# Scores of the first two groups moved into the input products of three attentions, and the conv taps cut in four

## The chip, the cores and the metric

The kernel runs on one core of a Trainium2 chip. The metric is the device time of one execution in microseconds; lower is better. Each number of the trace comes from one profiled execution.

## The reference, cut to what matters

Two transformer blocks run one after the other on 256 rows of width 1024, all in float32. The first has a sliding-window attention beside a differential one, a cross attention over a memory of 256 rows, and a feed-forward net. The second has two layers with modulation from a condition vector; layer 0 mixes a short convolution with a latent attention (MLA), layer 1 is a sparse attention with three branches (NSA). The three attentions that the change touches:

```python
def cross_attention(h, m, w_q, w_kv, w_o):
    q = (h @ w_q).reshape(Bn, S, CROSS_HEADS, CROSS_HEAD_DIM)        # 4 heads of 256
    ...
    s = jnp.einsum('bshd,bmhd->bhsm', q, k) * CROSS_HEAD_DIM ** -0.5
    p = jax.nn.softmax(s, axis=-1)

# MLA: 8 heads, 64 + 32 columns, causal; beside it the short convolution
u, gate_c, gate_b, cq, ckv, kr = jnp.split(h @ w_in, ...)
y_conv = gate_b * short_conv(gate_c * u, conv_w)                      # 3 taps, 512 channels

# NSA: 16 heads of 64, three branches
return gb[..., 0:1] * o_c + gb[..., 1:2] * o_s + gb[..., 2:3] * o_w   # compressed, selected, window
```

## The kernel before, in words

Everything of size runs on TensorE as a product of split numbers: each weight unit (128 x 2048, 1 MB) is loaded by DMA into `raw`, ScalarE copies it into a rounded high part `whi` (`split_hi`, L1101), VectorE subtracts it to get the low part `wlo` (`split_lo`, L1118), and `three` (L1162 to L1164) does three matmuls for each product. There are three such buffers (four in some stages), and a unit is split two or three units ahead of its use. While the products run, VectorE also forms the modulation vectors (`ada_terms`, L2175 and L2181): eight partial sums per part of `ada_w`, held in the buffers of `qT` and `pT`, and TensorE adds them over the partitions (`ada_out`, L1309).

The order of work on each engine is fixed by a list of stages that `make_plan` writes. Every engine walks the same list and issues its own part of each stage; engines wait for each other through semaphores only, so whatever stands behind a waiting instruction waits too. `linear` writes a product x @ w unit by unit; its argument `inner` hangs stages behind a unit. `T` counts the rounds of a pair of PSUM banks in which TensorE transposes (`turn`, L1166 to L1171, four transposes of 128 x 128 a round); a round needs the bank of the round before last emptied, by ScalarE ("A", L1806) or VectorE ("D", L2257).

An attention works in groups of heads and query rows. For each group TensorE computes scores (L1422 cross, L1426 MLA, L1437 NSA, L1414 compressed) into one of two pairs of banks, VectorE takes the row maxima (`smax`, L2292 to L2301; for NSA it adds the mask first and copies the scores to SBUF), ScalarE the exponentials with their sums (`exps`, L1832), TensorE transposes the result (`turn_probs`), ScalarE copies it to `pT` (L1840), and TensorE multiplies with the values (L1491). The loop of `attend` (L1474) does in step i: scores of group i + 1, values of group i - 2, transposes of group i - 1, and then the stages that are nested at i. Groups use three buffers for their exponentials in turn (`probs`). Before the first scores TensorE waits until every round in the stage's list `turned` has been emptied.

Before the change the three attentions open like this. Cross: the query product `w_cq` runs (four units), the partial sums of the modulation end behind it, then all eight rounds of query and key transposes, then the loop. MLA: the input product has eight units, the last six for the convolution; query transposes stand behind unit 5, key transposes and the whole of `conv_taps` (L2417 to L2420: sixteen VectorE operations) behind unit 6, then unit 7 and the loop. NSA: behind unit 5 the hidden layer of the compressed keys and values (`cmp_hid`), behind unit 6 their transposes and half of the query rounds, behind unit 7 `cmp_out` (its two rounds are emptied by VectorE: `kcz` L2486, `kz` L2492) and the other half, then the loop.

## Time and profile before

| | us |
|---|---|
| three timed runs, median (lowest, highest) | 1523.01 (1517.4, 1527.09) |
| the profiled execution's own time | 1518.52 |
| its span, first to last instruction | 1516.7 |
| TensorE busy | 1456.2 (96%) |
| VectorE busy | 1053.7 (69%) |
| ScalarE busy | 729.2 (48%) |
| mean granted clock of TensorE | 0.990 |

Cross opens at some 207 us of the span, MLA at 712, NSA at 1216. In the rows below PE is TensorE, DVE is VectorE, ACT is ScalarE. A timeline row gives the start, the time taken, the engine and line, the operation, output<-input, and how many instructions are merged in it; in square brackets stands how long the engine was idle before it and what it waited for. An fp32 matmul of scores or values shows as two records.

### The profile page before, as it was taken

To read this page: it belongs to the slowest core of one execution; us is meant where nothing else is said; L and a number is where in the kernel's file an instruction comes from. 1 tells how busy PE (TensorE), PEld (TensorE's weight loads), DVE (VectorE), ACT (ScalarE), POOL (GpSimd) and SP (SyncE) were. 2 spreads that over 40 slices of the span, in tenths; PEclk is the share of its full clock that TensorE was granted. 3 is DMA by queue.
4 is the path that set the end of the run, shared out by engine and by line. 5 is a ranking of instruction groups with operands and counts; after the bars stand their busy time and mean duration, and the time that the engine had idled before them with its cause. 6 is when DMAs were issued, how large, how long until landed. Compare 5 with 4: busy or idle time off the path is not lost.

```text
span 1516.7 us, 18742 instructions
## 1 busy us (share of the span) xinstructions
PE 1456.2 (96%) x7206; PEld 1197.3 (79%) x7206; DVE 1053.7 (69%) x1432; ACT 729.2 (48%) x1101; POOL 75.9 (5%) x133
## 2 busy tenths in 40 slices
PE   8997999999999999998999999899999989999998
PEld 7885777888877888887778888688887867788886
DVE  4897565877777777666477767777777678775544
ACT  6545545444454434364464333544435765554342
POOL 7200000000000000010000000000000000000000
PEclk9999999999999999999999999999999999999999
DMA  8870434687856888634368888588883710566560
GB/s 299 281 249 29 167 111 167 232 302 270 272 189 220 302 271 273 225 123 161 105 234 290 280 264 274 171 281 270 284 280 121 243 46 1 180 193 202 188 208 28
DMA packets 189087, 314.21 MB, mean 207 GB/s; under 512 B 6896, under 2 KB 100440, under 8 KB 189000
## 3 DMA queue, kind: packets, MB, share of 16 engines
q1 hardware_dynamic: 148800, 232.87, 46.9%
q10 hardware_dynamic: 38408, 75.65, 13.7%
q0 software_dynamic: 1792, 4.51, 1.0%
q8 instruction: 58, 0.95, 0.3%
q14 instruction: 29, 0.24, 0.0%
HBM read 311.92 MB, written 1.07 MB: 206 GB/s over the span
## 4 chain that ended last, share of the span: by engine, by line
PE 82%; DVE 9%; ACT 5%; issue 3%; DMA 1%; POOL 1%; ACTq 0%; POOLq 0%; DVEq 0%
PE ps L1162 24%; PE ps L1164 24%; PE ps L1163 23%; PE ps L1171 5%; PE ps L1491 2%; PE ps L1309 2%; DVE wlo L1118 1%; PE ps L1437 1%; DVE rmax L2295 1%; ACT sp L1832 1%; DVE tmp L1986 1%; ACT whi L1101 1%; DVE xn L1933 1%; DVE x L1941 0%; DVE wide L1118 0%
## 5 line engine op out<-in xcount | busy, mean ns | idle before, releaser
L1118 DVE TENSOR_TENSOR wlo<-raw,whi 128x2048 fp32r<-128x2048 f32 (+2 forms) x168 | 381.4, 2273 | 153.1 <-ACT whi L1101 153.0
L1162 PE MATMUL ps<-whi,aT 128*128 128x512 f32 (+3 forms) x1000 | 400.5, 401 | 10.6 <-DVE aTl L1974 6.1
L1164 PE MATMUL ps<-wlo,aT 128*128 128x512 f32 (+3 forms) x1000 | 388.9, 389 | 0.0
L1163 PE MATMUL ps<-whi,aTl 128*128 128x512 f32 (+3 forms) x1000 | 387.7, 388 | 0.0
L1101 ACT ACTIVATE whi<-raw 128x2048 fp32r<-128x2048 f32 (+2 forms) x169 | 319.5, 1895 | 82.7 <-DVE prow L2181 35.9
L1162 PEld LDWEIGHTS ps<-whi,aT 128*128 128x128 f32 x1000 | 188.6, 189 | 54.1 <-issue 11.3
L1164 PEld LDWEIGHTS ps<-wlo,aT 128*128 128x128 f32 x1000 | 188.5, 188 | 39.8
L1163 PEld LDWEIGHTS ps<-whi,aTl 128*128 128x128 f32 x1000 | 189.2, 189 | 34.3
L1778 ACT ACTIVATE hT<-ps 128x256 fp32r<-128x256 f32 (+1 forms) x102 | 42.2, 414 | 340.6 <-PE ps L1171 172.4
L1162 PE MATMUL ps<-whi,hT 128*128 128x512 f32 (+1 forms) x364 | 141.1, 390 | 1.4 <-ACT z L1756 1.4
L1164 PE MATMUL ps<-wlo,hT 128*128 128x512 f32 (+1 forms) x364 | 138.4, 382 | 0.0
L1163 PE MATMUL ps<-whi,hTl 128*128 128x512 f32 (+1 forms) x364 | 138.1, 381 | 0.0
L1118 DVE TENSOR_TENSOR wide<-raw,wide 128x2048 fp32r<-128x2048 f32 (+1 forms) x46 | 104.4, 2269 | 31.6 <-ACT wide L1101 31.6
L1101 ACT ACTIVATE wide<-raw 128x2048 fp32r<-128x2048 f32 x45 | 86.2, 1916 | 13.3 <-DVE prow L2181 5.0
L2181 DVE SCALAR_TENSOR_TENSOR qT<-qT,cact 128x512 f32<-128x512 f32 x108 | 80.9, 749 | 2.6
L2228 DVE TENSOR_TENSOR hTl<-ps,hT 128x256 fp32r<-128x256 f32 (+1 forms) x102 | 46.7, 458 | 50.8 <-ACT hT L1778 50.8
L1794 ACT ACTIVATE sp<-ps 128x256 f32<-128x256 f32 x88 | 33.5, 382 | 96.9 <-PE ps L1164 96.9
L1162 PEld LDWEIGHTS ps<-whi,hT 128*128 128x128 f32 (+1 forms) x364 | 67.1, 184 | 15.5 <-issue 2.1
L1164 PEld LDWEIGHTS ps<-wlo,hT 128*128 128x128 f32 (+1 forms) x364 | 67.0, 184 | 14.2
L1162 PE MATMUL ps<-wide,aT 128*128 128x512 f32 (+1 forms) x184 | 74.2, 403 | 3.4 <-DVE aTl L1974 2.1
L1163 PEld LDWEIGHTS ps<-whi,hTl 128*128 128x128 f32 (+1 forms) x364 | 67.2, 185 | 12.7
L1162 PE MATMUL ps<-wide,hT 128*128 128x512 f32 (+1 forms) x192 | 73.3, 385 | 0.0
(271 smaller groups left out, 2030.3 us busy)
## 6 DMA issues: line engine op xcount, KB each, us to landing
raw<-in_ff_w SPq DMA_DIRECT2D x176, 512.0 KB, 4.8
raw<-in_ff_w SPq DMA_DIRECT2D x44, 1024.0 KB, 5.1
qT<-in_ada_w ACTq DMA_DIRECT2D x36, 1024.0 KB, 6.7
pT<-in_ada_w ACTq DMA_DIRECT2D x36, 1024.0 KB, 7.2
raw<-in_w_up SPq DMA_DIRECT2D x16, 1024.0 KB, 5.8
raw<-in_w_down SPq DMA_DIRECT2D x16, 1024.0 KB, 5.1
raw<-in_w_in SPq DMA_DIRECT2D x9, 1024.0 KB, 9.8
raw<-in_w_ckv SPq DMA_DIRECT2D x8, 1024.0 KB, 5.5
```

What stands on the lines that cost most here:

```text
L1101: act.activation(hi_of(u), raw_of(u), ACT.Copy).then_inc(w_hi, 1)
L1118: dve.tensor_tensor(lo_of(u), raw_of(u), hi_of(u).bitcast(F32), ALU.subtract).then_inc(w_lo, 1)
L1162: pe.matmul(out_ap, hi, w, start=start, stop=False)
L1163: pe.matmul(out_ap, lo, w, start=False, stop=False)
L1164: return pe.matmul(out_ap, hi, wl, start=False, stop=stop)
L1171: last = pe.transpose(tbank(t)[0:m, col:col + kp], src, ident[0:kp, 0:kp])
L1309: last = pe.matmul(tbank(t)[:, c:c + 1], asum[:, k * P:(k + 1) * P], ones[:, 0:1], start=True, stop=True)
L1491: last = pe.matmul(o[:, i * dv:(i + 1) * dv], pT[:, n % 2, i * g["nkc"] + kc, :], zt[:, kc, v0:v0 + dv], start=kc == 0, stop=kc == g["nkc" ...
L1778: act.activation(hT[:, e["base"]:e["base"] + nk, e["tt"] * P:(e["tt"] + 1) * P], tbank(e["t"])[:, 0:nk * P].rearrange("p (a b) -> p a b", ...
L1794: act.activation(part(tt)[:, 0:HB2], bank[:, 0:HB2], ACT.Silu).then_inc(r_ready, 1)
L2181: ins = dve.scalar_tensor_tensor(asum if q == KC - 1 else w, w, c, before, ALU.mult, ALU.add)
L2228: dve.tensor_tensor(hTl[:, k0:k0 + nk, to], tbank(e["t"])[:, 0:nk * P].rearrange("p (a b) -> p a b", b=P), hT[:, k0:k0 + nk, to].bitcast(F ...
```

## The change

It takes the scores, maxima and exponentials of the first groups out of the loop and hangs them into the input product as a stage of their own, `attend_head`. TensorE does the scores of groups 0 and 1 there, VectorE and ScalarE the maxima and exponentials of the first `ahead` groups: two in cross and MLA, one in NSA.

- Cross: two rounds of keys are turned behind unit 1 of `w_cq`; a round of keys, two of queries and the head behind unit 2; a round of keys and two of queries remain behind unit 3. The third buffer for exponentials moves to another part of `z`.
- MLA: queries and keys are turned together behind unit 5, the head stands behind unit 6. `conv_taps` is cut in four portions (product, first tap, second tap, third tap) nested at steps 0 to 3 of the loop; the gate moves from step 1 to step 3.
- NSA: groups alternate, two of the first 128 query rows and two of the last (heads 0 to 7, then 8 to 15). The first half of the queries is turned ahead of the hidden columns behind unit 6, with the head behind it; the second half moves into step 1 of the loop, and group 4 waits for it. Group 1 holds its exponentials in `gbc`.

```diff
-        self.keys_turned = r[-2:]
+        self.keys_turned = r
...
-    p.linear(A["w_cq"][0], D, D, "z", "w_cq", flush=3)
-    p.turned("qk_cross", 8, ["A", "D"] * 4)
-    attend("cross", list(p.keys_turned), A["w_co"][0], None, {4: first_half(), 5: early(0), 6: rest_then_early})
+    def cross_head():
+        cross_turn((0, 1), (2,))
+        attend_head("cross", cross, 2)
+
+    p.linear(A["w_cq"][0], D, D, "z", "w_cq", flush=3, inner={1: lambda: cross_turn((), (0, 1)), 2: cross_head})
+    cross_turn((2, 3), (3,))
+    attend("cross", cross, A["w_co"][0], None, {4: first_half(), 5: early(0), 6: rest_then_early})
...
-                     inner={1: latent_stats, 2: latent_norms, 3: ups, 4: pack, 5: turn_q, 6: turn_k_taps})
+                     inner={1: latent_stats, 2: latent_norms, 3: ups, 4: pack, 5: turn_q, 6: lambda: attend_head("mla", turned, 2)})
...
-                   {1: lambda: p.gate(layer, 5), 4: conv_last, 5: early(0), 6: rest_then_early})
+                   {0: taps(0), 1: taps(1), 2: taps(2), 3: taps_gate, 4: conv_last, 5: early(0), 6: rest_then_early})
...
             def turn_hid():
+                p.turned("q_nsa", 2, ["A", "D"], c0=0)
+                turned.extend(p.keys_turned)
                 r = p.rounds(2, "D")
                 p.stage("cmp_turn", rounds=r, hid=list(r_cmp))
-                p.turned("q_nsa", 2, ["A", "D"], c0=0)
-                turned.extend(p.keys_turned)
                 r_cmp[:] = r
+                attend_head("nsa", turned, 1)
...
                 p.stage("cmp_out", rounds=r, turned=list(r_cmp))
+                turned.extend(r)
...
+            def turn_q_rest():
                 p.turned("q_nsa", 2, ["A", "D"], c0=512)
-                turned.extend(r + p.keys_turned)
+                late[4] = p.keys_turned
...
-            spec += [dict(kind="nsa", br=br, t=t, h0=h, nh=4) for t in range(NT) for h in (0, 4, 8, 12)]
+            spec += [dict(kind="nsa", br=br, t=t, h0=h + h2, nh=4) for h in (0, 8) for t in range(NT) for h2 in (0, 4)]
...
-                scores(gs[0])
+                if not st.get("head"):
+                    scores(0)
+                if st["kind"] == "attend_head":
+                    scores(1)
+                    return
                 for i in range(len(gs) + 3):
-                    if i + 1 < len(gs):
-                        scores(gs[i + 1])
+                    if i + 1 < len(gs) and not (i == 0 and st["head"]):
+                        scores(i + 1)
...
+                if st["kind"] == "attend_head":
+                    for g in gs[0:st["ahead"]]:
+                        smax(g, None)
+                    return
```

VectorE in the query product of cross, before, from the second half of unit 2's work to the loop (`wlo` is the low part of a weight unit, `qT`, `pT`, `prow` the terms of the modulation or, as COPY, turned queries):

```order
L2181 SCALAR_TENSOR_TENSOR qT<-qT,cact 128x512 x3
L1118 TENSOR_TENSOR wlo<-raw,whi 128x2048
L2181 SCALAR_TENSOR_TENSOR pT<-pT,cact,qT 128x512
L2181 SCALAR_TENSOR_TENSOR pT<-pT,cact 128x512
L1118 TENSOR_TENSOR wlo<-raw,whi 128x2048
L2181 SCALAR_TENSOR_TENSOR pT<-pT,cact 128x512
L2181 SCALAR_TENSOR_TENSOR prow<-pT,cact 128x512
L2188 TENSOR_TENSOR mod<-ps,prm 128x2 x2
L2257 COPY qT<-ps 128x512 x2
L2257 COPY kz<-ps 128x512 x2
L2295 TENSOR_REDUCE rmax<-ps 128x2
```

The same place in the changed kernel:

```order
L2235 SCALAR_TENSOR_TENSOR qT<-qT,cact 128x512 x3
L2311 COPY kz<-ps 128x512
L1152 TENSOR_TENSOR wlo<-raw,whi 128x2048
L2235 SCALAR_TENSOR_TENSOR pT<-pT,cact,qT 128x512
L2235 SCALAR_TENSOR_TENSOR pT<-pT,cact 128x512
L2311 COPY qT<-ps 128x512
L2349 TENSOR_REDUCE rmax<-ps 128x2
L2355 TENSOR_SCALAR negm<-rmax 128x2
L2349 TENSOR_REDUCE rmax<-ps 128x2
L2355 TENSOR_SCALAR negm<-rmax 128x2
L1152 TENSOR_TENSOR wlo<-raw,whi 128x2048
L2235 SCALAR_TENSOR_TENSOR pT<-pT,cact 128x512
```

One copy of keys, one of queries and the maxima of groups 0 and 1 now stand ahead of the last low part and the last two terms of the modulation.

VectorE in NSA, before, from the last split ahead of unit 7 to group 0 (`hidc`: hidden columns, `kcz` and `kz` 15x64: compressed keys and values):

```order
L1118 TENSOR_TENSOR wide<-raw,wide 128x2048
L2477 COPY hidc<-ps 128x32 x2
L2257 COPY qT<-ps 128x512
L1118 TENSOR_TENSOR wlo<-raw,whi 128x2048
L2486 COPY kcz<-ps 64x15 x4
L2492 COPY kz<-ps 15x64 x8
L2257 COPY qT<-ps 128x512
L2292 TENSOR_TENSOR sp<-ps,causal 128x4x128
L2295 TENSOR_REDUCE rmax<-sp 128x4
```

The same place in the changed kernel, to group 1 (in `gbc`):

```order
L1152 TENSOR_TENSOR wide<-raw,wide 128x2048
L2311 COPY qT<-ps 128x512
L2540 COPY hidc<-ps 128x32 x2
L2346 TENSOR_TENSOR sp<-ps,causal 128x4x128
L2349 TENSOR_REDUCE rmax<-sp 128x4
L2355 TENSOR_SCALAR negm<-rmax 128x4
L1152 TENSOR_TENSOR wlo<-raw,whi 128x2048
L2549 COPY kcz<-ps 64x15 x4
L2555 COPY kz<-ps 15x64 x8
L2346 TENSOR_TENSOR gbc<-ps,causal 128x4x128
```

Group 0's maximum now stands ahead of the low part, and the compressed keys and values behind it. On TensorE the head's scores stand between the hidden columns and unit 7, and group 2's scores follow `cmp_out` at once.

ScalarE in MLA, from the query copies to group 2, before:

```order
L1806 ACTIVATE qT<-ps 96x512 x2
L1101 ACTIVATE whi<-raw 128x2048
L1806 ACTIVATE kz<-ps 96x512 x2
L1101 ACTIVATE whi<-raw 128x2048
L1756 ACTIVATE zc<-ps 128x512 x2
L1832 ACT_TABLE_LOAD
L1832 ACTIVATE sp,sums<-ps,negm 128x128 x8
L1840 ACTIVATE pT<-ps 128x512
```

And in the changed kernel:

```order
L1856 ACTIVATE qT<-ps 96x512 x2
L1856 ACTIVATE kz<-ps 96x512 x2
L1135 ACTIVATE whi<-raw 128x2048
L1882 ACT_TABLE_LOAD
L1882 ACTIVATE sp,sums<-ps,negm 128x128 x8
L1135 ACTIVATE whi<-raw 128x2048
L1806 ACTIVATE zc<-ps 128x512 x2
L1890 ACTIVATE pT<-ps 128x512
```

The eight exponentials of groups 0 and 1 now stand ahead of the last high part and of the copies of unit 7's result.

## Rows read from the trace of the kernel before

**Rows 1.** The page: the span, and the busy time of each engine.
```profile
span 1516.7 us, 18742 instructions
PE 1456.2 (96%) x7206; PEld 1197.3 (79%) x7206; DVE 1053.7 (69%) x1432; ACT 729.2 (48%) x1101; POOL 75.9 (5%) x133
```

**Rows 2.** Table of stretches: length, busy time of each engine; PEclk: granted clock.
```profile
core 0: us, PE busy (x) PEld busy (x) DVE busy (x) ACT busy (x) POOL busy (x), PEclk, DMA share, GB/s
209.00:212.60 3.60, 3.60 (x18) 2.75 (x16) 1.35 (x2) 1.20 (x2) 0.00 (x0) 0.53 0.52 199
...
719.00:721.00 2.00, 1.19 (x3) 1.01 (x4) 0.35 (x2) 2.00 (x13) 0.00 (x0) 0.50 0.86 304
...
1221.00:1223.00 2.00, 2.00 (x6) 1.55 (x6) 0.12 (x1) 0.00 (x0) 0.00 (x0) 0.50 0.00 0
```

**Rows 3.** Timelines of the cross opening: TensorE, then VectorE, then ScalarE.
```profile
195.25 0.50 PE L1162 MATMUL ps<-whi,aT 128*128 128x512 f32 x1
...
207.60 1.05 PE L1309 MATMUL ps<-ones,prow 128*128 128x1 f32 x8 [1.16 <-DVE prow L2181]
...
215.61 3.69 PE L1422 MATMUL ps<-kz,qT 128*128 128x256 f32 x16 [0.83 <-issue]
219.74 1.99 PE L1422 MATMUL ps<-kz,qT 128*128 128x256 f32 x8 [0.44 <-ACT z L1832]
...
197.91 2.33 DVE L2181 SCALAR_TENSOR_TENSOR qT<-qT,cact 128x512 f32<-128x512 f32 x3
...
206.79 0.75 DVE L2181 SCALAR_TENSOR_TENSOR prow<-pT,cact 128x512 f32<-128x512 f32 x1
...
210.04 0.69 DVE L2257 COPY qT<-ps 128x512 f32<-128x512 f32 x1 [1.19 <-PE ps L1171]
...
217.68 0.69 DVE L2295 TENSOR_REDUCE rmax<-ps 128x2 f32<-128x512 f32 x1 [2.17 <-PE ps L1422]
...
201.10 1.92 ACT L1101 ACTIVATE whi<-raw 128x2048 fp32r<-128x2048 f32 x1 [3.31 <-PE ps L1164]
...
218.67 0.48 ACT L1832 ACTIVATE z<-ps,negm 128x256 f32<-128x256 f32 x1 [3.98 <-DVE negm L2301]
```

**Rows 4.** Timelines of the MLA opening: TensorE, then VectorE, then ScalarE.
```profile
712.68 0.61 PE L1426 MATMUL ps<-kz,qT 96*128 96x128 f32 x4
...
719.81 2.08 PE L1426 MATMUL ps<-kz,qT 96*128 96x256 f32 x4 [4.70 <-ACT sp L1832]
...
724.70 1.03 PE L1426 MATMUL ps<-kz,qT 96*128 96x256 f32 x4
...
737.60 0.47 PE L1162 MATMUL ps<-whi,aT 128*128 128x512 f32 x1 [0.28 <-DVE aTl L2428]
...
709.19 1.15 DVE L2418 TENSOR_SCALAR zc<-tmp,prm 128x256 f32<-128x256 f32 x4
710.37 3.37 DVE L2420 SCALAR_TENSOR_TENSOR zc<-tmp,prm,zc 128x255 f32<-128x255 f32 x8
...
724.06 1.22 DVE L2295 TENSOR_REDUCE rmax<-ps 128x4 f32<-128x1024 f32 x1 [3.88 <-PE ps L1448]
...
716.96 1.28 ACT L1832 ACT_TABLE_LOAD   x1 [3.48 <-DVE negm L2301]
...
725.52 0.47 ACT L1832 ACTIVATE zc<-ps,negm 128x256 f32<-128x256 f32 x1
```

**Rows 5.** Timelines of the NSA opening: TensorE, then VectorE, then ScalarE.
```profile
1215.98 0.30 PE L1557 MATMUL ps<-hidc,w2s 128*128 128x30 f32 x2
...
1220.72 5.46 PE L1437 MATMUL ps<-kz,qT 128*128 128x256 f32 x12 [1.09 <-DVE qT L2257]
...
1231.08 1.45 PE L1437 MATMUL ps<-kz,qT 128*128 128x512 f32 x3
...
1207.04 2.29 DVE L1118 TENSOR_TENSOR wide<-raw,wide 128x2048 fp32r<-128x2048 f32 x1 [0.42 <-ACT wide L1101]
...
1217.08 1.81 DVE L2492 COPY kz<-ps 15x64 f32<-15x64 f32 x8
...
1224.57 1.28 ACT L1832 ACT_TABLE_LOAD   x1 [6.12 <-DVE negm L2301]
```

More of the change, by code:

```diff
@@ L570, in make_plan, with attend_head, attend @@
     out = []
-    def attend(which, turned, w, gate, nest, k0=0):
-        groups = attention_groups(p, which)
+    heads = {}
+    def attend_head(which, turned, ahead):
+        heads[which] = dict(groups=attention_groups(p, which), ahead=ahead)
+        p.stage("attend_head", which=which, turned=list(turned), **heads[which])
+    def attend(which, turned, w, gate, nest, k0=0, late=None):
+        head = heads.get(which, dict(ahead=0))
+        groups = head.get("groups") or attention_groups(p, which)
         out[:] = [dict(p.out_begin(w, gate, k0), half=groups[len(groups) // 2 - 1])]
-        p.stage("attend", which=which, turned=turned, groups=groups, nest=attention_turns(p, groups, nest))
+        p.stage("attend", which=which, turned=turned, groups=groups, nest=attention_turns(p, groups, nest),
+                head=which in heads, ahead=head["ahead"], late=late)
     def first_half(n=None):
@@ L605, in make_plan, with cross_turn @@
     p.edge(p.out_rest(out[0]), ("prm", G_CROSS), eps=1e-5)
-    p.linear(A["w_cq"][0], D, D, "z", "w_cq", flush=3)
-    p.turned("qk_cross", 8, ["A", "D"] * 4)
-    attend("cross", list(p.keys_turned), A["w_co"][0], None, {4: first_half(), 5: early(0), 6: rest_then_early})
+    cross = []
+    def cross_turn(qs, ks):
+        p.turned("qk_cross", len(qs) + len(ks), (["A", "D"] * 4)[0:len(qs) + len(ks)], qs=qs, ks=ks)
+        cross.extend(p.keys_turned)
+    def cross_head():
[4 more added lines that the diff above has]
+    attend("cross", cross, A["w_co"][0], None, {4: first_half(), 5: early(0), 6: rest_then_early})
     p.ada_every = (4,4)
@@ L645, in turn_q, with taps, taps_gate @@
                 turned.extend(p.keys_turned)
-            def turn_k_taps():
                 p.turned("k_mla", 4, ["A", "D"] * 2)
                 turned.extend(p.keys_turned)
-                p.stage("conv_taps", after=p.last_fill)
+            def taps(i):
+                return lambda: p.stage("conv_taps", after=after_in, phase=i)
+            def taps_gate():
+                taps(3)()
+                p.gate(layer, 5)
             def conv_last():
@@ L710, in finish_rest @@
                 early(1)()
-            attend("nsa", turned, A["nsa_w_out_2"][0], (p.n_gates + 1, 1.0), {2: lambda: p.gate(layer, 5), 21: finish, 22: finish_rest})
+            attend("nsa", turned, A["nsa_w_out_2"][0], (p.n_gates + 1, 1.0), {1: turn_q_rest, 2: lambda: p.gate(layer, 5), 21: finish, 22: finish_rest}, late=late)
             p.ada_until(35)
@@ L750, in attention_groups @@
     p.groups += spec
+    if which == "nsa":
+        spec[1]["second"] = True
     return spec
@@ L962, in build @@
         kfull = xn[:, :, 0:768]
-        third = {"swa": z[:, 0, 768:1792], "diff": z[:, 0, 768:1792], "mla": zc[:, 1, 1024:2048]}
+        third = {"swa": z[:, 0, 768:1792], "diff": z[:, 0, 768:1792], "mla": zc[:, 1, 1024:2048], "cross": z[:, 0, 1024:2048]}
         def probs(g):
             n = g["g"] % 3
+            if n == 2 and g.get("second"):
+                return gbc[:, :]
             return sp[:, n, :] if n < 2 else third.get(g["kind"], z[:, 0, 0:1024])
@@ L1026, in transposes @@
             elif kind == "qk_cross":
-                for r in range(4):
+                for r in st["ks"]:
+                    pair(zc, 256 * r, kz[:, 2 * r:2 * r + 2, :])
+                for r in st["qs"]:
                     pair(z, 256 * r, qT[:, 2 * r:2 * r + 2, :])
-                for r in range(4):
-                    pair(zc, 256 * r, kz[:, 2 * r:2 * r + 2, :])
             elif kind in ("q_mla", "k_mla"):
@@ L1403, in attend, with scores @@
                     pe.wait_ge(kz_zero, 1)
-                def scores(g):
+                def scores(i):
+                    g = gs[i]
+                    for t in (st.get("late") or {}).get(i, ()):
+                        wait_emptied(pe, T, lambda j: t)
                     n = g["g"]
@@ L2370, in attend @@
                 dve.wait_ge(t_ready, st["turned"][-1] + 1)
+                if st["kind"] == "attend_head":
+                    for g in gs[0:st["ahead"]]:
+                        smax(g, None)
+                    return
                 for i in range(len(gs) + 3):
-                    if i < len(gs):
+                    if st["ahead"] <= i < len(gs):
                         smax(gs[i], gs[i - 3] if i >= 3 else None)
@@ L2415, in each, with tap @@
                     dve.wait_ge(v_done, n)
-                each(lambda k, u, t, w: dve.tensor_tensor(t, zcf[:, 4 + k, :], u, ALU.mult))
-                each(lambda k, u, t, w: dve.tensor_scalar(u, t, w[2], None, ALU.mult))
-                for i in (1, 0):
+                def tap(i):
                     each(lambda k, u, t, w: dve.scalar_tensor_tensor(u[:, 2 - i:S], t[:, 0:S - 2 + i], w[i], u[:, 2 - i:S],
                                                                      ALU.mult, ALU.add))
+                if st["phase"] == 0:
+                    each(lambda k, u, t, w: dve.tensor_tensor(t, zcf[:, 4 + k, :], u, ALU.mult))
+                elif st["phase"] == 1:
+                    each(lambda k, u, t, w: dve.tensor_scalar(u, t, w[2], None, ALU.mult))
+                else:
+                    tap(3 - st["phase"])
             def conv(st):
```

16 lines of the change are left out of this document (12 added, 4 removed).

## The prediction, made before the changed kernel ran

> **What bounds the kernel now.** I read the page first: TensorE is busy 1456.2 us of a span of 1516.7 us, 96%, and VectorE 69% [rows 1]. So the end is set by TensorE, and a change of order can only win back its idle time (60.5 us in all) and the time in which its clock is granted at half. The second view was the table of stretches: in 719 to 721 us and 1221 to 1223 us the clock is 0.50, 1.2 GHz instead of 2.4 GHz, both times in the opening of an attention, and 0.53 in 209 to 212.6 us [rows 2]. Third, I read the timeline of the three openings engine by engine.
>
> In each opening TensorE has nothing but the first two groups' scores, and then waits for the chain maximum (VectorE), exponentials (ScalarE). I count what each loses against the work in it.
>
> - Cross: from the end of the last unit (206.4) to the scores of group 2 (219.74) are 13.3 us [rows 3] (206.4 is 207.60 less the 1.16 us that TensorE waited). Work: the four partial sums of the modulation behind the unit 0.95, eight rounds of transposes at some 0.52, two groups of scores 3.7, in all 8.8. Lost 4.5.
> - MLA: 712.68 to 724.7. 4.70 us idle before group 2's scores, and these run at half clock (four of their matmuls take 2.08 us, the same four of group 3 1.03) [rows 4]. Work at full clock 5.2. Lost 6.8.
> - NSA: 1215.98 to 1231.08, 15.1 us, with 7.9 of work at full clock. Lost 7.2 [rows 5]. The scores of three groups take 5.46 us there, mostly at half clock; a round of four transposes waits 1.1 us for the copies of the compressed values.
>
> Together 18.5 us: no more than this is there to win.
>
> **The change, part by part.** Nothing is computed more or less; the operations of TensorE, VectorE and ScalarE are the same in number and size (one split row apart), and so are the DMAs. What counts is where each stands in its queue, and the order of the changed kernel shows that. Each engine works in order, so I laid the durations of the rows along the new queues.
>
> *Cross.* TensorE now turns two rounds of keys after unit 1, and three rounds (a key, two queries) and two groups of scores after unit 2. But round q0 is emptied by VectorE, and there its copy stands behind a split and two partial sums. VectorE is through its three sums at 200.24 (197.91 + 2.33), then copy of keys 0.69, low part of a weight unit 2.29 (as in [rows 5]), two sums 1.5, copy of q0 0.69: 205.4 [rows 3]. TensorE began unit 2 at 195.25 and ended unit 3 at 206.4, some 5.5 us a unit; with the two rounds of keys ahead and the three behind, it stands at 203.4 and idles 2.2, then scores 3.69 (to 209.3) and unit 3 (to 214.75). Meanwhile ScalarE makes both groups' exponentials before the next high part: maximum of group 1 ready 210.4, exponentials 1.1, high part 1.92 (to 213.4), then on VectorE low part 2.29 and the last two sums 1.5: 217.3. TensorE waits for exactly these sums, so its wait of 1.16 becomes 2.6. It goes on at 217.4: partial sums 0.95, three rounds with a wait for a copy 1.9, the last copy 0.7, and group 2's scores start at 221.0 where they started at 219.74: **+1.3 us**. Ends: -4.5 if no wait is left, +2.8 if also one stretch at half clock falls on group 2's scores.
>
> *MLA and the taps.* Queries and keys are turned together (5.2 us for eight rounds instead of twice 2.2, since each pair waits for its copies), unit 6 follows to 707.7, scores of two groups to 710.1, unit 7 to 715.95. The maximum of group 0 is ready at 709.9, table load 1.28, eight exponentials 2.9 (four came between 718.24 and 719.7 before), to 714.15: TensorE does not wait for them, the 4.70 us are gone. But the high part comes after them (to 716.05) and its low part on VectorE until 718.45; then come taps portion 0 (1.45) and 1 (1.15) ahead of the maximum of group 2, though its scores are ready at 718.0. So that maximum runs 721.5 to 722.7 (1.22), and the exponentials start at 723.0 instead of 725.52: 2.5 us won, not 6.8. Portion 2 (1.67, half of the last taps row) stands ahead of group 3's maximum and takes 0.5 of it back, the later conv steps 0.2. The first product of the output comes at 735.75 instead of 737.60: **-1.85 us** [rows 4]. Ends: -6.8 (all of the loss) and 0 (a half-clock stretch in the sparse work between 722 and 730).
>
> *NSA.* Group 0's maximum and exponentials go ahead of unit 7's split on both engines. VectorE: split until 1209.33, copy of queries, hidden columns, then group 0 until 1213.2; ScalarE: table 1.28, exponentials 1.55, until 1216.1, and only then the high part (to 1218.0), which took place at 1210.74 before; low part to 1220.4, then the copies of the compressed keys and values, 0.7 + 1.81, to 1223.0. TensorE still waits for these two rounds before the first score after unit 7 (the list of rounds that the attention waits for holds them). It is through at 1218.6 and idles 4.4 us, to 1223.1. Then: group 2 (512 columns now) 1.88, turn, late queries, group 3; group 4 starts at 1230.8, against 1231.08, with 0.85 us more of scores done: 1.1 ahead. But the copy of the late queries stands before group 2's maximum on VectorE, 2.4 us idle there; 1.22 + 1.22 + 0.17 later, and 1.95 of exponentials and 0.6 of evacuation, TensorE has waited 1.65, and 0.9 for group 3. Net **+1.6 us**. The order of groups (two with 128 keys, two with 256) sums to the same on every engine; VectorE needs some 3.5 us for a long group (two passes of 1.22 and the small ones) against 3.1 on TensorE, and catches up in the short ones: 0, at most +1. The clock: after 4.70 us idle the MLA opening ran at half, so I take that for 4.4 us too, and it falls on group 2's scores (1.88 becomes 3.75): **+1.9 us**, ends 0 and +3. Ends for all of NSA: -7.2 and +5.5.
>
> *Rest.* The gate's transpose moves later by one group; its row is needed only at the edge, some 15 us on: 0. The larger wait lists are passed at once: 0. Weight loads may start later, in cross by up to 10 us, as splits do; no wait of ScalarE in [rows 3] is for a load, and the DMA share is 0.52 there and 0.00 in NSA [rows 2], so they have room: 0.
>
> Sum: 1.3 - 1.85 + 1.6 + 1.9 = **+3.0 us** (2.95).
>
> At the clock one rule is to be weighed. In 209 to 212.6 TensorE is busy 3.60 of 3.60 us, all in transposes, and granted 0.53 [rows 2]. The Trainium skill ("TensorE: Matmul & The Clock Gate", Part 4: PE-mode transpose) says that transposes don't count as activity for the clock in the way matmuls do; the trace agrees. By that rule the wait of 2.6 us in cross, with three rounds of transposes behind it, is one low stretch, which then falls on full scores rather than on transposes that wait for copies anyway. By it the sum would be some +1.9 more, +4.9; without it the +3.0 stands.
>
> **The rivals.**
> 1. *The waits go.* VectorE and ScalarE take the new work between splits as gaps allow and the openings lose most of their 18.5 us; I put it at 13, so 1507.8. For it: both engines idle in the input products (ScalarE 3.31 us before 201.10). Against it: their queues are fixed, and the exponentials stand ahead of the splits.
> 2. *Nothing arrives:* the shifts cancel within 1 us, 1520.8.
> 3. *Slower, by the clock.* The waits now lie between products, so that half-clock stretches fall on full-width work. One stretch costs 1.8 (3.6 us long at 0.53, [rows 2]) to 3.4 us (6.8 long, as in MLA, 717.7 to 724.5). Where cross, MLA and NSA each get one that they didn't have, +6 to +9, taken as 9: 1529.8. It decides from an idle of about 2.6 us in cross on; for it speaks the 0.53 after 1.16 us idle and transposes; against it, that the matmuls of unit 3 lie close before.
>
> **How the numbers follow.** The profiled execution took 1518.52 us (1516.7 span and 1.8 around it); the three timed runs have their median at 1523.01, so one run scatters by some 5 us. I start from the middle of the two, 1520.8, and add 3.0: **1523.8 us**. Forecast 0.55, its own range 1517 to 1529; rival 1 0.2, rival 2 0.1, rival 3 0.15. The range reaches to 1511 (most of rival 1) and 1531 (rival 3). A measurement of this kernel tells about 1% (15 us) from no change. Rival 1 would need 15 of its 18.5 to pass that: faster 0.04; rival 3 with bad runs: slower 0.03; same 0.93.
>
> **What would show it.** Right: in cross a wait of TensorE for VectorE's copy of q0 ahead of group 0's scores, and a longer one at the partial sums; in MLA no wait before group 2's scores, but one of 2 us or more later for its exponentials; in NSA a wait of 4 us for the copies of compressed values with a low clock behind. Wrong: output products that start over 5 us earlier in MLA or NSA, or no low clock at 1223.

## The result, and the profile after

The changed kernel takes 1534.33 us (median of nine runs, 1529.10 to 1537.09) against 1521.37 us of the kernel before (nine runs, 1516.93 to 1527.09). The ratio is 1.0085, 95% interval [1.0068, 1.0101]: 13 us slower. The profiled execution took 1532.78 us, with a span of 1531.0 us (before: 1518.52 and 1516.7). The forecast was 1523.8, and its range ended at 1531. In the table of experiments the row of e7 leaves out one of its seven runs, which took 1639.98 us at a mean granted clock of 0.849, far below the others.

| section of the profile (TensorE) | before | after | forecast |
|---|---|---|---|
| cross and the feed-forward net behind it, from the first query product to the next attention's input product | 268.46 | 271.85 (+3.4) | +1.3 |
| MLA, from the end of the latent part to the product behind the output | 80.80 | 81.42 (+0.6) | -1.85 |
| NSA, from its first transposes to the product behind the output | 135.06 | 145.25 (+10.2) | +3.5 |

The three make 14.2 of the span's 14.3 us. The page of the changed kernel:

```profile
span 1531.0 us, 18772 instructions
PE 1466.2 (96%) x7206; PEld 1207.4 (79%) x7206; DVE 1052.8 (69%) x1431; ACT 729.6 (48%) x1102; POOL 76.6 (5%) x133
```

Against [rows 1] VectorE and ScalarE do the same. TensorE is busy 10.0 us more, with the same 7206 matmuls: they ran longer, and the mean granted clock is lower (0.981 against 0.990). Idle time grew by 4.3 us. The sections in the table of stretches, of before and then of after (the columns are those of [rows 2]):

```profile
185.90:454.36 268.46, 262.61 (x1240) 215.16 (x1241) 188.92 (x223) 126.24 (x162) 5.10 (x11) 0.99 0.65 221
683.29:764.09 80.80, 71.84 (x456) 63.76 (x456) 49.11 (x82) 37.92 (x72) 4.59 (x7) 0.94 0.43 147
1184.38:1319.44 135.06, 123.15 (x755) 99.42 (x756) 103.19 (x225) 82.03 (x211) 2.17 (x4) 0.97 0.30 102
```
```profile
186.32:458.17 271.85, 263.31 (x1240) 216.00 (x1241) 188.18 (x222) 126.53 (x163) 5.09 (x11) 0.99 0.64 218
687.04:768.46 81.42, 74.93 (x455) 66.83 (x456) 48.74 (x82) 38.03 (x72) 4.59 (x7) 0.90 0.44 147
1188.53:1333.78 145.25, 129.92 (x756) 105.88 (x756) 103.36 (x225) 82.14 (x211) 2.17 (x4) 0.92 0.28 95
```

The granted clock fell from 0.94 to 0.90 in MLA and from 0.97 to 0.92 in NSA. Where it fell, by short stretches of the changed kernel:

```profile
219.00:226.00 7.00, 5.90 (x19) 4.45 (x18) 1.60 (x4) 0.98 (x2) 0.00 (x0) 0.51 0.18 68
727.00:745.00 18.00, 15.21 (x63) 13.74 (x64) 10.58 (x20) 8.84 (x22) 3.58 (x5) 0.53 0.09 30
1225.00:1233.00 8.00, 6.04 (x17) 3.67 (x18) 3.47 (x14) 2.79 (x10) 0.00 (x0) 0.57 0.41 131
1239.00:1243.00 4.00, 3.89 (x18) 3.72 (x19) 3.59 (x13) 3.43 (x13) 1.16 (x2) 0.58 0.06 22
1287.00:1291.00 4.00, 4.00 (x24) 4.00 (x24) 2.78 (x11) 0.64 (x2) 0.00 (x0) 0.57 0.02 4
1301.00:1312.00 11.00, 9.81 (x28) 7.50 (x29) 7.01 (x11) 3.38 (x4) 0.00 (x0) 0.53 0.02 3
```

In [rows 2] such stretches lay in the same three openings, but shorter: here one runs 18 us through MLA's loop, and three more stand late in NSA, where before had none. The kernel before had one more behind MLA's loop, on wide products alone, and in NSA the stretch of [rows 2] is 8 us long in all:

```profile
738.00:742.00 4.00, 4.00 (x12) 3.15 (x11) 2.63 (x2) 0.00 (x0) 0.00 (x0) 0.57 0.07 18
1219.00:1227.00 8.00, 6.10 (x16) 4.23 (x16) 3.79 (x7) 2.41 (x7) 0.00 (x0) 0.57 0.07 23
```

Both kernels also have a stretch of 4 us at 980 to 987 us, outside the three sections. TensorE's timeline of the changed kernel shows what it did ahead of each:

```profile
205.86 3.69 PE L1459 MATMUL ps<-kz,qT 128*128 128x256 f32 x16 [1.06 <-DVE qT L2311]
217.17 1.05 PE L1343 MATMUL ps<-ones,prow 128*128 128x1 f32 x8 [2.13 <-DVE prow L2235]
221.44 3.75 PE L1459 MATMUL ps<-kz,qT 128*128 128x256 f32 x8 [0.88 <-ACT qT L1856]
...
728.69 1.97 PE L1528 MATMUL ps<-z,pT 128*128 128x64 f32 x8 [3.61 <-ACT pT L1890]
739.19 3.65 PE L1528 MATMUL ps<-z,pT 128*128 128x64 f32 x16 [0.73 <-ACT pT L1890]
742.59 0.77 PE L1196 MATMUL ps<-whi,aT 128*128 128x512 f32 x1
...
1226.96 3.75 PE L1474 MATMUL ps<-kz,qT 128*128 128x512 f32 x4 [4.89 <-DVE kz L2555]
1239.11 1.54 PE L1528 MATMUL ps<-z,pT 128*128 128x64 f32 x8 [1.99 <-ACT pT L1890]
1257.74 1.97 PE L1528 MATMUL ps<-z,pT 128*128 128x64 f32 x16 [1.01 <-ACT pT L1890]
1286.44 2.77 PE L1528 MATMUL ps<-z,pT 128*128 128x64 f32 x16 [1.06 <-ACT pT L1890]
```

Against [rows 3] the wait for the partial sums went from 1.16 to 2.13 us, and a wait of 1.06 for q0's copy is new. Against [rows 4] the 4.70 us ahead of group 2's scores are gone, and 3.61 us stand at group 1's values. Against [rows 5] 4.89 us are new at the copies of the compressed values, and group 2's scores (3.75 us; 1.88 at full clock) run behind them at half. The engines behind MLA's wait, VectorE and then ScalarE:

```profile
721.84 1.42 DVE L2480 TENSOR_TENSOR tmp<-zc 128x256 f32<-128x256 f32 x4
723.59 1.13 DVE L2482 TENSOR_SCALAR zc<-tmp,prm 128x256 f32<-128x256 f32 x4
724.75 1.23 DVE L2349 TENSOR_REDUCE rmax<-ps 128x4 f32<-128x1024 f32 x1
726.22 0.47 ACT L1882 ACTIVATE zc<-ps,negm 128x256 f32<-128x256 f32 x1 [3.70 <-DVE negm L2355]
```

Two portions of the taps stand ahead of group 2's maximum, and ScalarE idles 3.70 us for it.

The time follows the clock from run to run too: of the nine runs the fastest (1529.10 us) had a mean granted clock of 0.986 and the slowest (1537.09) 0.976, 8.0 us for 0.010. In e17 below it is 13.9 us for 0.014 (1517.69 to 1531.56, 0.997 to 0.983). The change's mean clock is 0.008 below that of the kernel before (0.980 and 0.988), so an estimate from these slopes gives the clock 6 to 8 of the 13 us, and 5 to 7 to time that would be lost at an equal clock too.

### The profile page after: what moved, and what is told of

It reads as the page before. It is cut to its first block, busy times and chain, and to the rows that moved or that the text cites. A ratio compares the mean times of both kernels' runs of the same rounds, so it can differ in the third digit from the quotient of the medians.

```text
span 1531.0 us, 18772 instructions
## 1 busy us (share of the span) xinstructions
PE 1466.2 (96%) x7206; PEld 1207.4 (79%) x7206; DVE 1052.8 (69%) x1431; ACT 729.6 (48%) x1102; POOL 76.6 (5%) x133
## 3 DMA queue, kind: packets, MB, share of 16 engines
HBM read 311.92 MB, written 1.07 MB: 204 GB/s over the span
## 4 chain that ended last, share of the span: by engine, by line
PE 84%; DVE 8%; ACT 4%; issue 2%; POOL 1%; DMA 0%; ACTq 0%; POOLq 0%; DVEq 0%
PE ps L1196 24%; PE ps L1198 24%; PE ps L1197 24%; PE ps L1205 5%; PE ps L1528 2%; PE ps L1343 2%; PE ps L1474 1%; DVE wlo L1152 1%; DVE rmax L2349 1%; ACT whi L1135 1%; ACT sp L1882 1%; DVE tmp L2040 1%; PE ps L1459 1%; DVE xn L1987 1%; ACT pT L1890 1%
## 5 line engine op out<-in xcount | busy, mean ns | idle before, releaser
L1196 PE MATMUL ps<-whi,aT 128*128 128x512 f32 (+3 forms) x1000 | 400.5, 401 | 10.3 <-DVE aTl L2028 6.1
L1198 PEld LDWEIGHTS ps<-wlo,hT 128*128 128x128 f32 (+1 forms) x364 | 67.1, 184 | 14.2
```

Source lines behind the costliest of these rows:

```text
L1196: pe.matmul(out_ap, hi, w, start=start, stop=False)
L1198: return pe.matmul(out_ap, hi, wl, start=False, stop=stop)
```

## The experiments

"Clock" is the mean of the granted clock over a kernel's runs; the kernel before had 0.988, the changed one 0.980. Ratios are to the kernel before on the same chip (medians 1520.40 to 1521.62).

| kernel | what it is | median us | ratio [95%] | clock |
|---|---|---|---|---|
| e1 | cross part alone | 1522.36 | 1.0011 [0.9998, 1.0025] | 0.987 |
| e2 | MLA part alone | 1520.55 | 0.9998 [0.9986, 1.0010] | 0.986 |
| e3 | NSA part alone | 1530.87 | 1.0045 [1.0015, 1.0074] | 0.983 |
| e4 | NSA's order of groups alone | 1525.88 | 1.0031 [1.0013, 1.0048] | 0.985 |
| e5 | change, compressed copies waited for late | 1531.54 | 1.0069 [1.0044, 1.0093] | 0.981 |
| e6 | change, old order of groups | 1526.47 | 1.0041 [1.0027, 1.0054] | 0.982 |
| e7 | change, idle matmuls 4, 7, 9 | 1532.15 | 1.0070 [1.0044, 1.0095] | 0.988 |
| e17 | change, idle matmuls 2, 4, 5 | 1523.63 | 1.0020 [0.9999, 1.0041] | 0.991 |
| e8 | MLA part, 7 idle matmuls | 1517.32 | 0.9979 [0.9964, 0.9993] | 0.991 |
| e16 | MLA part, 4 | 1518.31 | 0.9978 [0.9966, 0.9990] | 0.990 |
| e10 | MLA part, 24 transposes instead | 1520.15 | 0.9997 [0.9978, 1.0016] | 0.988 |
| e9 | before, 10 idle matmuls in MLA | 1520.52 | 1.0001 [0.9989, 1.0013] | 0.991 |
| e15 | before, 5 | 1517.47 | 0.9973 [0.9958, 0.9988] | 0.990 |
| e13 | MLA part, taps whole | 1519.54 | 0.9987 [0.9973, 1.0000] | 0.986 |
| e12 | MLA part, taps whole, 2 idle matmuls | 1513.55 | 0.9956 [0.9941, 0.9972] | 0.993 |
| e11 | as e12, three more fillings | 1513.05 | 0.9962 [0.9947, 0.9977] | 0.994 |
| e14 | change, old order, taps whole | 1526.28 | 1.0028 [1.0013, 1.0043] | 0.983 |
| e18 | as e14, idle matmuls 2, 2, 5 | 1514.23 | 0.9951 [0.9933, 0.9968] | 0.994 |

### Each part alone: e1, e2, e3, e4

The other attentions stand as before in each. e4 keeps only this line of the change:

```diff
+            spec += [dict(kind="nsa", br=br, t=t, h0=h + h2, nh=4) for h in (0, 8) for t in range(NT) for h2 in (0, 4)]
```

> Only the cross part of the change (two rounds of keys behind unit 1, the head behind unit 2, the third buffer moved); MLA and NSA stand as before. In the changed kernel everything behind cross is 3.8 us later than before. Theory A (the loss is TensorE's clock: waits in front of sparse work bring stretches at half clock): about +3.8 us in the profiled execution, with a stretch of some 6 us at 0.50 that begins at the wait for the last partial sums. Theory B (the loss is queueing alone): +1.3 to +1.7 us, scores of group 2 at 221.4, and no low clock beyond that of before. Theory C (where the clock falls depends on the whole program's timing and not on this place): anything from -2 to +5, with low stretches at other places than in the changed kernel.

> Only the MLA part (queries and keys turned together, head behind unit 6, taps in four portions); cross and NSA as before. In the changed kernel this part costs 0.6 us by the profile: 4.70 us of waiting went, 3.61 us at the first values came, and the stretch at half clock grew from some 10.5 to 16.5 us. Theory A (clock): +0.6 us, one long low stretch behind a wait for pT. Theory B (queueing alone, my forecast): -1.85 us. Theory C (chance of timing): between -3 and +3, with the low stretches elsewhere.

> Only the NSA part (order of groups, head, late queries); cross and MLA as before. In the changed kernel it costs 10 us by the profile. Theory A (clock): +10 us, the wait of 4.9 us for the compressed keys and values followed by low clock, and low clock again behind the waits of about 1 us for pT and at the end of the compressed branch. Theory B (queueing alone, my forecast): +1.6 to +3.5. Theory C (chance): the opening as forecast, but no low clock in the last 20 us of the attention, +3 to +5.

> Only the order of NSA's groups (two with 128 keys, two with 256), with no head and no late queries; all else as before. Theory A1 (the order itself is a cost: VectorE is late after two long groups, TensorE waits 1.0 us three times, and low clock follows): +3 to +7 us. Theory A2 (the head with its wait of 4.9 us is the cost and the order is free, as forecast): 0 to +1 us. Where e3 less e4 is near 0 the order is all of it.

Cross costs about 1.7 us and MLA nothing, both within their intervals of no change; NSA costs 6.8. The order of groups by itself costs 4.7 us: A1, not the "0, at most +1" of the forecast. Each part alone brings its own low stretch in its profile: 223 to 230 us at 0.51 in e1, 726 to 737 at 0.53 in e2. (The three ratios make 1.0054 and the whole is 1.0085; e3's interval is too wide to say whether the parts add up.) One part of the order's time is waits; TensorE, VectorE, ScalarE of e4 at the second pair of long groups:

```profile
1243.67 1.00 PE L1508 MATMUL ps<-z,pT 128*128 128x64 f32 x8
1245.87 1.10 PE L1508 MATMUL ps<-z,pT 128*128 128x64 f32 x8
1249.73 1.97 PE L1508 MATMUL ps<-z,pT 128*128 128x64 f32 x16 [1.01 <-ACT pT L1870]
...
1243.87 1.23 DVE L2326 TENSOR_TENSOR z<-ps,causal 128x1024 f32<-128x1024 f32 x1 [0.38 <-PE ps L1454]
1254.34 1.23 DVE L2326 TENSOR_TENSOR z<-ps,causal 128x1024 f32<-128x1024 f32 x1 [1.69 <-PE ps L1454]
...
1248.58 1.05 ACT L1870 ACTIVATE pT<-ps 128x512 f32<-128x512 f32 x2
```

The values that stand beside a long group's maximum in a step are those of the group two steps earlier. In the old order these are long too (1.97 us) from the third long group on; in pairs they are the short ones (1.00, 1.10), so TensorE is done early, while VectorE's maximum and ScalarE's exponentials of the second long group still run and ScalarE's copies of the turned probabilities stand behind them, until 1249.6. TensorE waits 1.01 us. Then VectorE waits 1.69 us for scores: both engines lose in turn. Three such waits (1.01, 1.01, 1.07) and two of 1.16 and 0.77 at the first pair stand in e4, against 0.49, 0.34, 0.22 and 0.21 us at values in the kernel before. That is not all of the 4.7 us. NSA's section in e4, and a stretch of it that the kernel before doesn't have:

```profile
1183.94:1322.22 138.28, 125.03 (x755) 100.41 (x756) 103.34 (x225) 81.94 (x211) 2.17 (x4) 0.96 0.29 99
1266.00:1270.00 4.00, 4.00 (x13) 2.44 (x12) 1.69 (x7) 2.73 (x10) 0.00 (x0) 0.57 0.00 0
```

Against 135.06 us with 123.15 busy before, TensorE idles 1.3 us more, since a wait of 1.38 us at the first turned probabilities is gone, and is busy 1.9 us more, by the clock. This execution is the fastest of e4's twelve; over the runs the mean clock is 0.003 lower than before, some 3 us at their slope (1521.26 to 1534.08 us for 0.990 to 0.978, 10.7 for 0.010). So 1.5 to 2 of the 4.7 us are waits and the rest is the clock again, as an estimate.

### The change with one thing mended: e5, e6

```diff
-                turned.extend(r)
+                late[16] = r
```

for e5, and for e6 the old list of groups with the late queries nested at step 0 (`late[2]`).

> The changed kernel, but the two rounds of compressed keys and values are waited for at the first compressed group (group 16) and no longer before group 2's scores, which don't read them. Theory A (this wait of 4.89 us is one of the costs): group 2's scores start 4.9 us earlier, TensorE then waits at the next turn (its bank still holds those values) for the rest, some 1.2 to 3 us; what goes is the time of one long group's scores, 1.9 us, and with it part of the low clock behind: -2 to -4 us against the changed kernel's mean of 1533.8, so 1530 to 1532. Theory B (the wait only moves, the order of groups is the cost): within 1 us of 1533.8.

> The changed kernel with NSA's groups in the old order (four with 128 keys, then four with 256), head and late queries kept (the late queries are turned one step sooner, since group 2 needs them). Theory A1 (order costs 4.7 us on average as it did alone): 1529 to 1530, no waits of 1.0 us for pT at the three later places, and no low clock in the last 20 us of the attention. Theory A2 (with the head in place the order is no cost, since the head needs two short groups at its start, not alternation): within 1 us of 1533.8. Theory B (late queries now stand ahead of group 2's scores, and their copies behind group 1's maximum on VectorE): a new wait of 2 us or more there, so 1532 or above.

e5 is 2.3 us below the changed kernel's 1533.8, by means 1531.5 of six runs with 3.6 us of scatter, so unclear. Its profile shows the wait of 4.89 us gone, and waits of 0.93, 1.22 and 3.15 us at three later places: most of it only moved. e6 goes from 1.0085 to 1.0041, 6.7 us: the order is the largest single cost, and more than I expected of A1. Its mean clock rises by 0.002 only (0.980 to 0.982), some 2 us, so most of the 6.7 comes at an equal clock: with the head in place the order costs more time in waits than alone. A wait of 5.01 us for the compressed values is still there.

### Is it the clock? Idle matmuls: e7, e8, e9, e10

Matmuls whose result is overwritten were put into waits of TensorE. They compute nothing that is used; TensorE still waits for the same things.

```diff
+            def fill(bank, n):
+                for _ in range(n):
+                    pe.matmul(bank, qT[0:96, 0, 0:P], kz[0:96, 0:2, :].rearrange("p a b -> p (a b)"), start=True, stop=True)
...
+                    if kind == "mla" and g is gs[0]:
+                        wait_free(pe, U, lambda j: f)
+                        fill(ubank(f), 7)
```

In MLA they stand ahead of group 0's values, one step before the wait of 3.61 us at group 1's.

> The changed kernel with idle matmuls put into three waits of TensorE, so that it works instead of idling while it waits for the same things: 4 (128x512) before cross's last partial sums (wait 2.13 us), 7 before MLA's first values (3.61 us), 9 before NSA's group 2 (4.89 us). Their results are overwritten. Theory A (idle TensorE in front of sparse work is what lowers the clock): the mean granted clock rises from 0.980 to 0.985 or more and the mean time falls from 1533.8 by 4 to 6 us, though nothing else is done earlier. Theory B (the time is lost in the queues, the clock is a bystander): 0 to +1 us, as the matmuls fill waits only. Theory C (low stretches come from the kind of work, transposes and small matmuls, whatever stands before): clock unchanged, 0 to +1 us.

> Only the MLA part of the change on the kernel before (as e2_mla), with the 7 idle matmuls ahead of the first values. e2_mla by itself was at 1521.06 on average, 0.15 below before; at an equal clock it was 1.6 us faster and its clock gave 1.5 back. Theory A (clock): 1519.0 to 1520.0, so 1.2 to 2.2 us faster than before (1521.2), with the stretch of 0.50 behind the wait shorter. Theory B: as e2_mla, within 0.7 us of 1521.1.

> The kernel before, with 10 idle matmuls (128x512, overwritten later) where TensorE waits 4.70 us ahead of MLA's group 2 scores; nothing else. From the kernel before, MLA from the end of its latent part to the product behind it takes 80.80 us in the profiled execution, with 10.5 us at half clock; with head, taps and idle matmuls (e8) it takes 78.44. Theory A (the gain of e8 is the clock alone, the moved work gives nothing): about 78 to 78.5 us there and 1518 in all, like e8. Theory B (about half and half: the head takes the wait away, the idle matmuls keep the clock): 79 to 80 us, 1519 to 1520.5. Theory C (idle matmuls before work at 96 rows don't help): 80.8, 1521.

> As e8 (MLA part only), but TensorE fills the wait of 3.6 us ahead of the first values with 24 transposes (of 96x128) instead of 7 matmuls. In the kernel before, 209 to 212.6 us was all transposes and at half clock. Theory A (being busy is enough): as e8, 1517.5 to 1518.5, clock 0.991, no stretch at 0.50 behind the wait. Theory B (transposes don't keep the clock up): as e2_mla, 1520.5 to 1522, clock 0.986 to 0.988, and a stretch of 0.50 over the first values and turned probabilities.

e8 is faster than before, by 3.2 us, where the same kernel without idle matmuls (e2) was even. But e7 gained little (1.0070 against 1.0085, with intervals that overlap) and e9 nothing, with clocks of 0.988 and 0.991. The timeline of e9 shows why:

```profile
715.50 8.75 PE L1200 MATMUL ps<-kz,qT 96*128 96x512 f32 x20
724.09 1.03 PE L1454 MATMUL ps<-kz,qT 96*128 96x256 f32 x4
```

The ten matmuls are twenty records and take 8.6 us, 0.86 each; I had read a row of four records as four matmuls. So e9's ran 4 us past its wait of 4.70 (group 2's scores start at 724.09), and e7's and e8's ran past theirs too. In e7's profile the three filled places are at full clock, but a stretch behind them, late in NSA, is longer than in the changed kernel:

```profile
1288.00:1309.00 21.00, 19.22 (x71) 15.90 (x69) 12.28 (x39) 4.04 (x11) 0.00 (x0) 0.51 0.00 0
```

The group was made again with the right length. e10 doesn't decide: its transposes took 2.15 us and left waits of 1.61 and 1.43, its profile has 0.57 from 732 to 744 us, and its runs scatter from 1512 to 1527.

### Idle matmuls of the right length: e15, e16, e17

The same edits with 5 (e15, in place of e9's 10), 4 (e16, of e8's 7), and 2, 4, 5 (e17, of e7's 4, 7, 9).

> As e9_beffill with 5 idle matmuls instead of 10. In e9's profile one took 0.86 us (two records), so its ten ran 4.3 us past the wait of 4.70; five take 4.3. MLA's section: before 80.80, e9 80.57. Theory A (the clock alone is worth the gain of the other kernels, no moved work is needed): 80.57 - 4.3 = 76.3 us in the section, 1516 to 1517.5 in all. Theory B (in the kernel before TensorE isn't the bound at that place, half clock costs nothing there): 80 to 80.8, 1520 to 1521.5.

> As e8_mlafill (MLA part as the change has it, taps in portions) with 4 idle matmuls (3.4 us) instead of 7 (6.0 us) in the wait of 3.6 us. MLA's section was 78.44 us in e8. Theory A (e8's matmuls overran by 2.4 us, which was lost): 76 to 76.3, 1515 to 1516.5; the taps' portions then cost 1.8 us against e12's 74.28. Theory B (the whole difference of 4.2 us between e8 and e12 is the taps'): 78 to 78.5, 1517.5 to 1518.5.

> The whole change with idle matmuls of the right length in three waits: 2 in cross (1.7 of 2.13 us), 4 in MLA (3.4 of 3.61), 5 in NSA (4.3 of 4.89); e7 had 4, 7 and 9, which ran 1.3, 2.4 and 2.8 us past the waits. Theory A (clock): 6.5 us below e7's 1532.0 (the overruns), so 1525 to 1527, against 1533.8 for the change. Theory B: not below 1530.

e17 is the whole change, with every wait for another engine left in, and 10 us below it (1.0020 against 1.0085). Its profile has no half clock in the three sections:

```profile
685.85:762.21 76.36, 71.66 (x464) 62.18 (x464) 48.76 (x82) 37.88 (x72) 4.58 (x7) 1.00 0.46 156
187.71:456.97 269.26, 262.46 (x1245) 214.87 (x1245) 188.25 (x222) 126.45 (x163) 5.09 (x11) 1.00 0.66 220
1182.51:1320.48 137.97, 124.58 (x765) 99.91 (x766) 103.15 (x225) 81.53 (x211) 2.17 (x4) 1.00 0.30 100
```

483.59 us, where the changed kernel had 498.52: 14.9 us are the clock's, 5.1 in MLA, 2.6 in cross, 7.3 in NSA. This is one execution; its runs reach from 1517.69 to 1531.56, with clocks of 0.997 to 0.983, so a low stretch still comes in some. Only NSA's opening was filled; that this execution has none of the later stretches, which e7 had, may be luck. e15 answers the question on the kernel before: it loses 3.8 us to half clock in MLA (80.80 to 76.98), and five idle matmuls alone win 0.27% [0.12, 0.42], though Theory A's number for the section (76.3) was a little low. e16's profile had a low stretch from 731 to 742 all the same (section 80.26), so its section doesn't tell; by its ratio (0.9978 and 0.9979) it is e8's equal, and the 2 us that a filling of the right length should have won didn't show. For the portions of the taps e17 stands in: the same MLA code, at full clock, took 76.36.

### The taps, and what is left: e12, e13, e11, e14, e18

```diff
+            def head_taps():
+                attend_head("mla", turned, 2)
+                for i in range(4):
+                    p.stage("conv_taps", after=p.last_fill, phase=i)
```

> As e8 (MLA part and idle matmuls), but the sixteen operations of the taps stand whole behind the head instead of in portions in the loop, where two of them (2.6 us) are ahead of group 2's maximum on VectorE; 2 idle matmuls instead of 7, since the wait they fill should shrink. VectorE has from about 710 to 716 us free there, while ScalarE makes exponentials and the high part. Theory A (the portions in the loop hold back group 2): the first values come 2 to 2.6 us earlier, 1515 to 1516.5. Theory B (taps whole run late and hold the last low part, so unit 7 of the input product waits): 1518 to 1521.

> As e12 (MLA part, taps whole behind the head), without the 2 idle matmuls. MLA's section (from the first product of the latent part's end to the product behind the attention) took 74.28 us in e12, 78.44 in e8, 80.88 in e2_mla, 80.80 before. Theory A (with the taps out of the way the wait is short and the idle matmuls do nothing): 74 to 75 us there, 1513 to 1515 in all. Theory B (without them a wait of about 1 us ahead of the first values brings a stretch at half clock, as in e2_mla): 76 to 78 us, 1516 to 1518.

e12 is faster than the kernel before by 0.44% [0.28, 0.59], 6.7 us, and e13, which differs from it by two matmuls alone, by 0.13% [0, 0.27]. TensorE in MLA's loop, e13 and then e12:

```profile
723.73 1.00 PE L1510 MATMUL ps<-z,pT 128*128 128x64 f32 x8
726.94 1.45 PE L1510 MATMUL ps<-z,pT 128*128 128x64 f32 x8 [1.77 <-ACT pT L1872]
728.18 1.91 PE L1187 MATMUL ps<-ident,zc 128*128 128x128 f32 x8
730.83 3.65 PE L1510 MATMUL ps<-z,pT 128*128 128x64 f32 x16 [0.73 <-ACT pT L1872]
```
```profile
719.27 1.88 PE L1202 MATMUL ps<-qT 96*128 96x512 f32 x4
720.99 1.00 PE L1520 MATMUL ps<-z,pT 128*128 128x64 f32 x8
723.12 1.10 PE L1520 MATMUL ps<-z,pT 128*128 128x64 f32 x8 [0.69 <-ACT pT L1882]
724.06 1.04 PE L1187 MATMUL ps<-ident,zc 128*128 128x128 f32 x8
725.96 1.97 PE L1520 MATMUL ps<-z,pT 128*128 128x64 f32 x16 [0.86 <-ACT pT L1882]
```

The wait of 1.77 us became 1.88 us of idle work (two matmuls, four records) and 0.69; behind it eight transposes take 1.04 us instead of 1.91 and sixteen records of values 1.97 instead of 3.65. The section is 80.24 us in e13 and 74.28 in e12. Both, and that of e15:

```profile
687.02:767.26 80.24, 75.23 (x455) 67.04 (x456) 49.49 (x82) 37.96 (x72) 4.59 (x7) 0.89 0.43 148
682.57:756.85 74.28, 69.83 (x459) 61.41 (x460) 49.63 (x82) 37.71 (x72) 4.58 (x7) 1.00 0.48 160
685.76:762.74 76.98, 72.33 (x466) 62.57 (x466) 49.12 (x82) 37.92 (x72) 4.58 (x7) 1.00 0.45 154
```

Two matmuls in a wait win 6.0 us there in the profiled executions (4.7 by the ratios). At full clock, MLA's section is 76.98 with the code of before (e15, its idle matmuls within the old wait), 76.36 with head and portions (e17) and 74.28 with head and whole taps (e12). So in these executions the portions gave away 2.1 of the 2.7 us that the head can win.

> As e12, with idle matmuls at three more waits of the kernel before: 8 small ones (128x128) ahead of the last partial sums in cross (1.16 us), 8 ahead of the opening of NSA's loop (1.09 us) and 10 ahead of the first turned probabilities there (1.38 us). Theory A (any wait ahead of sparse work lowers the clock, and short fillings prevent it): 2 to 4 us below e12, clock up by 0.003 or more. Theory B (the stretch in cross is made by transposes and not by the wait ahead of them, and NSA's by several short waits that one filling can't cure): within 1 us of e12.

> The whole change with two mends: NSA's groups in the old order (as e6, 1526.9 against 1520.9 of before beside it) and the taps whole behind MLA's head (as e12, but no idle matmuls). If the parts add up: +6.0 from e6, less the 4 to 6.5 us that e12 showed for whole taps, so between 0.5 us below and 2 us above before. Theory B (what the taps win in MLA is lost again later, since cross and the opening of NSA set where low clock falls): 4 us or more above before.

> The whole change as mended in e14 (old order of NSA's groups, taps whole; +4.3 us against before beside it), with 2, 2 and 5 idle matmuls in the same three waits. If the clock is what is left of the loss: MLA gives 6 us (as between e13 and e12), cross 1.5 to 2, NSA's opening 1 to 2, so 5 us below before or better, 1513 to 1516. If NSA's low stretches at the compressed branch stay: 1517 to 1520.

e11 is e12's equal: filling three short waits more shows no gain. e14 has ratio 1.0028, 2 us lower than e6's; whole taps without idle matmuls had given 1.7 on their own (e13 against e2), so the parts add up there, and the 4 to 6.5 us that I had expected don't come without idle matmuls. e18 adds nine idle matmuls to e14 and goes from 1.0028 to 0.9951, 11.7 us, as fast as e12 within the intervals; its mean clock rises from 0.983 to 0.994. The cross and NSA heads bring nothing beyond it.

## Why the prediction was wrong, point by point

- **The waits and starts were right.** Shifted by how much later each section begins (0.4, 3.75 and 4.15 us): cross, group 2's scores forecast at 221.0, measured 221.44, of which 0.42 is the shift; MLA, exponentials of group 2 forecast at 723.0 + 3.75 = 726.75, measured 726.22; NSA, group 2's scores forecast at 1223.1 + 4.15 = 1227.25, measured 1226.96. The waits of 2.6, 2 or more and 4.4 us came as 2.13, 3.61 and 4.89; q0's copy was awaited for 1.06 us, not 2.2. In cross at full clock (e17's 269.26 against 267.62, which is e4's section, with cross's code of before and no half clock in it) the step costs 1.6, forecast 1.3.
- **The step that failed is the clock's term in the sum,** "+1.9 us, ends 0 and +3", given to one stretch in NSA. The change loses 14.9 us to half clock in its profile (e17), of which the kernel before loses 3.8 in MLA (e15) and some 0.8 in cross (268.46 against e4's 267.62) as well, and in NSA up to 2.6 (6.10 us of work at 0.57): so 7.7 to 10.3 us are new, against 1.9. The runs' mean clocks give 6 to 8. I let only a wait as long as 4.4 us bring half clock, and priced it at the scores behind it. A wait of 2.13 in cross was enough, and in MLA the clock stayed low through the loop for 18 us; in both places half clock stood in the upper ends of the range (+2.8 and 0) and with nothing in the sum. The forecast -1.85 in MLA held at the exponentials, and was lost behind them: the output product was due at 735.75 + 3.75 = 739.50 and came at 742.59.
- **NSA's order, "0, at most +1", was mis-sized too:** e4 measures 4.7 us, e6 6.7, in part waits and in part the clock behind them. That short groups let VectorE catch up was the wrong argument. Busy times that sum to the same don't cost the same where TensorE's and VectorE's long phases lie two steps apart.
- **The waits were under-priced as well.** Without the clock's term the sum was +1.05 (1.3 - 1.85 + 1.6). e17 is still 3.0 us above the kernel before, though its own clock is the higher one (0.991 against 0.988); at an equal clock it would be some 5 to 6 above. In the profiles the excess lies in NSA (137.97 against 135.06), where the order belongs.
- **The other sum, +4.9,** with one low stretch in cross at +1.9 more, fits cross itself (3.2 forecast by it, 3.4 measured). That transposes are the reason is not shown (e10).
- **"All of the loss" in the openings, 18.5 us, was no bound.** Half clock reaches past the openings: in the kernel before it is there at 738 to 742 us, 13 us behind MLA's. The upper ends of the three parts, +2.8, 0 and +5.5, were all passed (+3.4, +0.6, +10.2).
- **Rival 3** (slower, by the clock, +9, 1529.8, chance 0.15) is nearest to what happened: its mechanism, in its three places, for more than half of the 13 us. Its size was capped by lengths of stretches read from one profile, and it left out the stretches at 1239, 1287 and 1301, the last two of which stand 60 us behind the change's opening. I gave it 0.15 because matmuls of unit 3 lie close before the wait in cross; they didn't keep the clock (0.51 from 219 us on).
- **Faster, same, slower:** 0.93 lay on "within 1%", and 0.85% is within it. The range's upper end, 1531, was too low by 3.

What stays open: which of NSA's waits brings the low stretch at the compressed branch. In the profiled executions of e9, e11 and e15, with NSA's code of before, it is there as well (1291 to 1301 in e9), in that of the kernel before it isn't. Whether transposes in a wait keep the clock was not settled (e10).

## What to carry to other kernels

Where small matmuls and transposes follow a wait, price the wait by the half clock that may follow it, over everything up to the next wide product and the first microseconds of it, and not by its length (here 128x512 matmuls took 0.63 us each until 1311 us, and 0.39 after): two matmuls worth 1.9 us, put into a wait of 1.77 us, saved 4.7 us. Before work is moved to close waits, try the cheap test first: idle matmuls in the waits of the kernel as it is (e15, 3.2 us); size them by the time of a whole matmul, not of a record. And when groups of different length alternate, lay two engines' steps side by side instead of summing their busy times.

## What was not expected of the hardware

- Half clock with TensorE fully busy: 1287 to 1291 us has 4.00 of 4.00 us busy, all small values, transposes and scores, at 0.57; and in the kernel before 738 to 742 us, all 128x512 products, is at 0.57 too.
- The same kernel's runs differ with the clock: nine runs of the change, 0.976 to 0.986, and 1537.09 to 1529.10 us in the same order but for ties. Five runs of e18 lie within 1.8 us (1513.84 to 1515.64), with clocks of 0.994 and 0.995.
